# One block's weight panels in another order: four compression panels set between four recurrence panels, the compressed attention branch four panels later, and three openings and the last step rearranged

## The reference

```python
xn = rms_norm(x, norm1_w[l])
z = xn @ w_in[l]
(q, k_c, v_c, k_s, v_s, k_w, v_w, g_nsa, xr, gr, g_a, g_b) = jnp.split(z, IN_SPLITS, axis=-1)
attn = nsa_attention(q, k_c, v_c, k_s, v_s, k_w, v_w, gates, pos_k, pos_v, ck_w1, ck_w2, cv_w1, cv_w2)
rnn = rg_lru_branch(xr, gr, conv_w, conv_b, w_a, b_a, w_i, b_i, lam)
merged = sigmoid(g_a) * (attn @ w_up_attn) + sigmoid(g_b) * (rnn @ w_up_rnn)
x = x + merged @ w_out
x = x + square(relu(rms_norm(x, norm2_w) @ mlp_w1)) @ mlp_w2
```

## Time and profile before

| quantity | value |
|---|---|
| median of 3 runs | 981.76 us (981.12 to 982.61) |
| the profiled execution's own time | 982.4 us |
| its span | 980.6 us |
| PE busy | 956.8 us, 98% of the span |
| DVE busy | 657.8 us, 67% |
| ACT busy | 531.6 us, 54% |
| mean granted TensorE clock | 0.995 of full speed |

### The profile page before, as it was taken

How to read it: one execution, slowest core, us unless ns; L and a number is a source line. 1 busy time by engine, 2 the same in 40 slices (tenths; PEclk the granted TensorE clock), 3 DMA queues, 4 the chain that set the end, 5 groups by cost and what they waited for, 6 DMA issues and landing times.

```text
span 980.6 us, 15325 instructions
## 1 busy us (share of the span) xinstructions
PE 956.8 (98%) x6094; PEld 864.8 (88%) x6094; DVE 657.8 (67%) x841; ACT 531.6 (54%) x691; POOL 59.3 (6%) x92
## 2 busy tenths in 40 slices
PE   6999999999899999999999999999999999999997
PEld 6889999998788888888888888999999898888885
DVE  5976777865656655577656566868666676666664
ACT  6776668535444443475444445669663465454543
POOL 5000000000200000022221000100000020000000
PEclk9999999999899999999999999999999999999999
DMA  9773343655556565538676565454424556555541
GB/s 276 234 241 108 108 145 107 223 172 172 190 178 210 172 195 190 189 121 257 206 219 210 184 201 171 139 185 151 129 90 170 178 187 206 182 192 191 182 160 43
DMA packets 128674, 173.20 MB, mean 177 GB/s; under 512 B 3120, under 2 KB 111936, under 8 KB 128624
## 3 DMA queue, kind: packets, MB, share of 16 engines
q1 hardware_dynamic: 127232, 168.59, 53.8%
q0 software_dynamic: 1392, 3.91, 1.3%
HBM read 171.43 MB, written 1.05 MB: 176 GB/s over the span
## 4 chain that ended last, share of the span: by engine, by line
PE 53%; DVE 1%; ACT 0%; POOL 0%; issue 0%; POOLq 0%; ACTq 0%; DVEq 0%
PE pair L647 15%; PE pair L650 8%; PE acc L617 5%; PE acc L619 5%; PE acc L618 5%; PE pair L617 4%; PE pair L618 4%; PE pair L619 4%; PE acc L1072 1%; PE acc L1056 1%; PE acc L1048 0%; PE acc L1047 0%; POOL rstd L495 0%; DVE xt L1860 0%; PE pair L703 0%; PE pair L699 0%
## 5 line engine op out<-in xcount | busy, mean ns | idle before, releaser
L647 PE MATMUL pair<-actp,wh 128*128 128x512 f32 x912 | 295.0, 398 | 2.9 <-DVE arena L1890 2.7
L1556 DVE TENSOR_TENSOR wl<-raw,wh 128x2048 fp32r<-128x2048 f32 x89 | 203.8, 2290 | 68.4 <-ACT wh L1170 68.3
L1170 ACT ACTIVATE wh<-raw 128x2048 fp32r<-128x2048 f32 x88 | 168.3, 1912 | 85.7 <-PE acc L619 85.7
L650 PEld LDWEIGHTS pair<-actp,wl 128*128 128x128 f32 x912 | 172.7, 189 | 40.3
L617 PE MATMUL pair<-actp,wh 128*128 128x256 f32 x648 | 186.0, 287 | 1.0 <-DVE arena L1734 0.9
L618 PE MATMUL pair<-actp,wh 128*128 128x256 f32 x648 | 183.3, 283 | 0.0
L619 PE MATMUL pair<-actp,wl 128*128 128x256 f32 x648 | 183.2, 283 | 0.0
L650 PE MATMUL pair<-actp,wl 128*128 128x256 f32 x912 | 180.3, 279 | 0.0
L1164 ACT ACTIVATE wh<-raw 128x2048 fp32r<-128x2048 f32 x69 | 132.1, 1914 | 84.6 <-PE pair L619 57.3
L1551 DVE TENSOR_TENSOR wl<-raw,wh 128x2048 fp32r<-128x2048 f32 x68 | 155.5, 2288 | 32.6 <-ACT wh L1164 32.2
L647 PEld LDWEIGHTS pair<-actp,wh 128*128 128x128 f32 x912 | 142.9, 190 | 4.7 <-DVE wl L1551 2.9
(11 more groups left out here) (295 smaller groups left out, 1130.8 us busy)
## 6 DMA issues: line engine op xcount, KB each, us to landing
raw<-in_w_in SPq DMA_DIRECT2D x37, 1024.0 KB, 5.3
raw<-in_mlp_w SPq DMA_DIRECT2D x32, 1024.0 KB, 5.3
raw<-in_ffn_w_gate SPq DMA_DIRECT2D x22, 1024.0 KB, 5.3
raw<-in_ffn_w_up SPq DMA_DIRECT2D x22, 1024.0 KB, 5.3
raw<-in_ffn_w_down SPq DMA_DIRECT2D x22, 1024.0 KB, 5.0
raw<-in_w_out SPq DMA_DIRECT2D x8, 1024.0 KB, 4.9
raw<-in_w_up_rnn SPq DMA_DIRECT2D x4, 1024.0 KB, 5.1
raw<-in_cmp_k_w SPq DMA_DIRECT2D x2, 1024.0 KB, 7.3
```

Source lines behind the costliest of these rows:

```text
L647: return nc.tensor.matmul(bank[:, :].rearrange("p (u t) -> p u t", u=2), h[:, k, cs], actp[:, :, k, :], **kw)
L650: return nc.tensor.matmul(bank[:, 0:T], l[:, k, cs], acth[:, k, :], **kw)
L1170: nc.scalar.activation(wh[:, n % R, :], raw[:, n % R, :], ACT.Copy).then_inc(hi_ready, 1)
L1556: nc.vector.tensor_tensor(wl[:, n % R, :], raw[:, n % R, :], wh[:, n % R, :].bitcast(F32), ALU.subtract).then_inc(lo_ready, 1)
```

## The change

Block 1's panels 5 to 12 become XR, CK, XR, CK, XR, CV, XR, CV: a long one and a short one in turn. The heads stay at the same panel numbers (`HEADS` = 5), and so do the convolution and the recurrence (`CONV` = 12). The compressed branch moves from 9 to `CHAIN` = 13, each of its steps four panels later, and its output buffers move with it (`vblk` to `hidt`, `pc` and `pcT` elsewhere). The transposes of `atok` and the split of their result move from GA + 1 and GA + 2 to GB + 1 and GB + 2. On VectorE `lo(4)` moves behind `flat`, `lo(5)` behind the split of `flat`, `lo(6)` and `lo(7)` together at n = 5, `queries_lo` of the first half ahead of the constants of the recurrence, and three memsets go from n = 0 to n = 13 and 15.

Outside block 1: at the MLP's opening the copy stands ahead of `lo(ML + 2)`; `spread(3)` stands in the middle of panel QKV2 + 1; in the weighted `residual` the two early `norm_lo` stand behind the last half; in the last step ScalarE takes all four squares first, VectorE scales the tokens' halves 1 and 3 (the last one in one instruction from `xt`), ScalarE scales 0 and 2 and issues one output DMA.

The core of the diff:

```diff
-Q, KCVC, KSVS, KWVW, CK, CV, XR, GRP, GA, GB = 0, 2, 3, 4, 5, 7, 9, 13, 17, 21
+Q, KCVC, KSVS, KWVW, HEADS, GRP, GA, GB = 0, 2, 3, 4, 5, 13, 17, 21
+XRS, CMPS = (5, 7, 9, 11), (6, 8, 10, 12)
+CONV, CHAIN = 12, 13
...
-                if CK <= n < XR:
+                if n in CMPS:
...
-                if CK <= n < CK + NH:
-                    head_score(n - CK)
-                if n == CK:
+                if HEADS <= n < HEADS + NH:
+                    head_score(n - HEADS)
+                if n == HEADS:
...
-                if n in (XR + 6, XR + 7):
-
-                    tt = n - XR - 6
+                if n in (CHAIN + 6, CHAIN + 7):
+
+                    tt = n - CHAIN - 6
                     pe.wait_ge(pcT_ready, 1)
                     if tt:
                         pe.wait_ge(oc_read, 1)
...
-                if n == GA + 1:
+                if n == GB + 1:
                     pe.wait_ge(normed, NH)
...
             first_panel(QKV2, [FIRST2[:, c, :] for c in range(2)], 3)
-            spread(3)
...
                     if c == 1:
                         m.then_inc(panel_done, 1)
+                    elif n == QKV2 + 1:
+                        spread(3)
...
-            square_sum(5, apart=True, result=True)
...
+            square_sum(5, apart=True)
+            result(0, 1)
+            result(2, 3)
+            act.wait_ge(out_ready[2], 1)
+            act.dma_start(out[0, P:2 * P, 0:512], xs[:, 1, 0:512]).then_inc(stored, 16)
...
+            split_at = {KCVC: [], KSVS: [KWVW], KWVW: [], KWVW + 1: [KWVW + 2, KWVW + 3]}
...
-                if n < ML - 1:
-                    lo(n + 2)
-                if n == Q + 1:
+                for m in split_at.get(n, [n + 2]):
+                    if m <= ML:
+                        lo(m)
+                if n == Q:
                     queries_lo(qT, 0, 1)
-                if n == Q:
                     lru_constants()
+                if n == CHAIN:
                     link(nc.vector.memset(pc[:, :, :, :], 0.0))
-                    link(nc.vector.memset(vblk[:, :, :, :], 0.0))
                     link(nc.vector.memset(kcd[:, :, :], 0.0))
...
-                if n in (XR + 7, XR + 8):
-                    tt = n - XR - 7
+                if n in (CHAIN + 7, CHAIN + 8):
+                    tt = n - CHAIN - 7
                     dve.wait_ge(oc_done, tt + 1)
                     nc.vector.tensor_tensor(atok[:, tt, :], atok[:, tt, :], ps[7][:, :], ALU.add).then_inc(oc_read, 1)
                     dve.wait_ge(oc_read, tt + 1)
...
-                        if then is not None:
+                        if then is not None and not weighted:
                             norm_lo(r, then, range(2))
...
-            lo(ML + 2)
             done(ML)
             nc.vector.tensor_copy(ffr, pair01[:, :, 0:T]).then_inc(ff_sum, 2)
+            lo(ML + 2)
...
-            residual(5, END - 1, weighted=True, scaled=4)
-            dve.wait_ge(y_ready, 8)
-
...
+            last_half(0)
+            last_weighted(0)
+            last_half(1)
+            last_weighted(1)
+            last_half(2)
+            last_half(3)
+            dve.wait_ge(y_ready, 4 + 2)
+            dve.wait_ge(rstd_ready, TT * 5 + 1)
+            _, right = half_row(1)
+            nc.vector.tensor_scalar(xs[:, 0, right], xs[:, 0, right], rstd[:, 0:1], None, ALU.mult).then_inc(out_ready[1], 1)
+            last_weighted(2)
+            dve.wait_ge(x_summed, 4 * 4 + 4)
             dve.wait_ge(rstd_ready, TT * 5 + 2)
```

More of the change, by code:

```diff
@@ L346, in build @@
         vb_ready = sem("vb_ready")
-        out_ready = [sem(f"out_ready{tt}") for tt in range(TT)]
+        out_ready = [sem(f"out_ready{b}") for b in range(2 * TT)]
         stored = sem("stored")
@@ L461, in _ @@
             load_ffn(F2, a["ffn2_w_gate_2"][0], a["ffn2_w_up_2"][0], a["ffn2_w_down_2"][0])
-            for b in range(2 * TT):
+            for b in (1, 0, 3):
                 tt, cs = half_row(b)
-                sp.wait_ge(out_ready[tt], b % 2 + 1)
+                sp.wait_ge(out_ready[b], 1)
                 sp.dma_start(out[0, tt * P:(tt + 1) * P, cs], xs[:, tt, cs]).then_inc(stored, 16)
@@ L797, in heads_between, with bank1 @@
             def heads_between(n):
[L799 to L802, removed]
+                if 0 <= n - HEADS - 3 < NH:
+                    head_mix(n - HEADS - 3)
+                if 0 <= n - HEADS - 2 < NH:
+                    head_turn(n - HEADS - 2)
+            def bank1(n):
+                return ps[1 - XRS.index(n) % 2] if n in XRS else ps[n % 2]
             def free_bank(n):
@@ L1170, in hi_in_loop, with square_sum @@
                     nc.scalar.activation(wh[:, n % R, :], raw[:, n % R, :], ACT.Copy).then_inc(hi_ready, 1)
-            def square_sum(r, weighted=False, apart=False, result=False, halves=range(2 * TT)):
+            def square_sum(r, weighted=False, apart=False, halves=range(2 * TT)):
                 for b in halves:
                     tt, cs = half_row(b)
-                    if result and b == 3:
-                        act.wait_ge(rstd_ready, TT * r + 1)
-                        act.wait_ge(y_ready, 4 + 2)
-                        for c in (0, 1):
-                            _, c0 = half_row(c)
-                            nc.scalar.activation(xs[:, 0, c0], xs[:, 0, c0], ACT.Copy,
-                                                 scale=rstd[:, 0:1]).then_inc(out_ready[0], 1)
                     if r:
@@ L1273, in _ @@
                 hi(n + 2)
-                k = n - CK - 1
+                k = n - HEADS - 1
                 if 0 <= k < NH:
@@ L1871, in residual @@
                 if then is not None:
-                    norm_lo(r, then, range(2, KT))
+                    norm_lo(r, then, range(0 if weighted else 2, KT))
             def hidden_lo(s):
@@ L2116, in _, with last_half, last_weighted @@
             swiglu(F2, F2_F)
-            residual(5, END - 1, weighted=True, scaled=4)
-            dve.wait_ge(y_ready, 8)
+            def last_half(b):
+                tt, cs = half_row(b)
+                if b < 3:
+                    dve.wait_ge(bank_done, 3 * 4 + b + 1)
+                else:
+                    done(END - 1)
+                nc.vector.scalar_tensor_tensor(xt[:, tt, cs], acc4[:, b, :], late[:, tt:tt + 1], xt[:, tt, cs],
+                                               ALU.mult, ALU.add).then_inc(x_summed, 1)
+            def last_weighted(b):
+                tt, cs = half_row(b)
+                dve.wait_ge(x_summed, 4 * 4 + b + 1)
+                nc.vector.tensor_tensor(xs[:, tt, cs], xt[:, tt, cs], fnb[:, cs], ALU.mult).then_inc(y_ready, 1)
+            dve.wait_ge(late_ready, TT * 4)
+            dve.wait_ge(fnb_loaded, 16 * 2)
+            last_half(0)
[10 more added lines that the diff above has]
+            dve.wait_ge(x_summed, 4 * 4 + 4)
             dve.wait_ge(rstd_ready, TT * 5 + 2)
-            for b in (2, 3):
-                tt, cs = half_row(b)
-                nc.vector.tensor_scalar(xs[:, tt, cs], xs[:, tt, cs], rstd[:, tt:tt + 1], None, ALU.mult).then_inc(out_ready[tt], 1)
+            nc.vector.scalar_tensor_tensor(xs[:, 1, right], xt[:, 1, right], rstd[:, 1:2], fnb[:, right], ALU.mult,
+                                           ALU.mult).then_inc(out_ready[3], 1)
 _INS = ["x", "w_in", "cmp_k_w1", "cmp_k_w2", "cmp_v_w1", "cmp_v_w2", "lru_w_a", "lru_w_i", "w_up_attn", "w_up_rnn",
```

110 lines of the change are left out of this document (59 added, 51 removed).

## The result

| | before | changed |
|---|---|---|
| median | 981.44 us (981.12 to 982.61, 4 runs) | 988.27 us (987.92 to 990.2, 4 runs) |
| the profiled execution's own time / span | 982.4 / 980.6 us | 988.5 / 986.7 us |
| mean granted clock in it | 0.995 | 0.994 |

The changed kernel is slower: the medians differ by 6.8 us (a ratio of 1.0070), and the ratio that goes with the 95% interval is 1.0077 (1.0062 to 1.0091). 987.2 us were forecast. In a second group of runs it took 988.42 us against 980.89 (1.0080, interval 1.0067 to 1.0094).

The account below looks back on a forecast made before the run. TensorE, busy 956.8 of 980.6 us, was taken as the bound, so only its idle and slow time counted. Terms summed to +5.45 on the 981.76 us median, giving 987.2 us; range 982.6 to 990.4.

Parts of the forecast that it names:

- opening of block 1: Block 1's opening: TensorE's waits of 0.9, 1.4, 0.7 and 0.5 us go, leaving about 0.1: -3.4 us.
- mixes in panels 10 and 12: Short panels 10 and 12: each mix waits for a norm, a 2.99 us chain against 0.95 of cover: +4.1 us.
- panel 15: Compressed branch at n = 14: `gelu` and two table changes delay ScalarE 2.4 us, partly absorbed: +1.2 us.
- the addition: Output at n = 20: TensorE waits for VectorE's addition, behind `recur(0)` and `lo(22)`: +5.9 us, bounds 0 and 8.
- clock behind it: After the addition's wait: a slow stretch as after the profiled 2.7 us wait, +3.0 us, bounds 0 and 3.4.
- rival C: Clock also falls in the head waits of panels 10 and 12, once or twice: 990.2 to 993.2 us; 15%.
- MLP's opening and the spread: MLP: copy first, TensorE starts 1.8 us earlier, no 3.0 us clock loss, -4.8; `spread(3)`: wait moves to score, -0.15.
- residual and last step: Weighted residual -0.1 us; last step up to -0.8, less 0.2 for GpSimd's root beside VectorE, -0.6.
- Rival A: VectorE reaches the output's addition in time, so 5.9 and 3.0 us go: 978.3 us; 8%.
- E: No head waits in panels 10 and 12, VectorE's chain being shorter than 2.99 us: 983.1 us; 5%.
- Rival B: Clock does not fall after the 5.9 us wait for the addition: 984.2 us; 7%.
- Rival D: The MLP's opening still runs slow, adding 3.0 us: 990.2 us; 5%.

Follow-up runs that it names:

- the run with the wait of panel 12 alone: Changed kernel with the norm ahead of the mask on VectorE in panel 10 only, panel 12 keeping its wait: 989.93 us (one run).
- bank 6: Changed kernel with the second half of the compressed output in bank 6, so TensorE need not wait for the addition: 981.81 us, 1.0006 of before.
- both edits: Changed kernel with the compressed output's second half in bank 6 and each head's norm ahead of the mask on VectorE: 975.45 us, 0.9941 of before.

## Why the prediction was right, and where not

The forecast was the addition's wait with its slow stretch, 987.2 us; measured 988.27. Term by term, in the profiled executions:

| term | predicted | found |
|---|---|---|
| opening of block 1 | -3.4 | -3.5, all four waits gone |
| mixes in panels 10 and 12 | +4.1 | +4.1 (matmuls 2.05 late each, of which 1.88 is listed as a wait) |
| panel 13 | +0.3 | 0 |
| panel 15 | +1.2 | +0.9 |
| the addition | +5.9 | +5.7, and 0.2 for the first half of the output |
| clock behind it | +3.0 | +2.0 |
| clock behind a head wait (rival C) | 0 | +1.7 |
| block 1 together | +11.1 | +11.1 |
| MLP's opening and the spread | -4.8 and -0.15 | -1.8 for the wait, -2.9 from there to the first score of block 2 |
| residual and last step | -0.7 | -0.4 |
| span | +5.45 | +6.1 |

That block 1 came to 11.1 both times is luck in part: -1.0 for the clock behind the addition and -0.7 in small terms were made up by +1.7 that the sum put at 0.

**The places were right**, and two were shown by taking away what waits: 7.3 us for the addition with its clock, 5.8 for the two mixes with theirs. Rival A (the addition in time) and E (no head waits) fall. Rival B falls too: the clock did drop. Rival D falls: in the changed kernel the MLP's opening ran at 1.00. Rival C came true once of twice; the step "I take 0" for waits of 2.0 us was too low, by 1.7, and the run with the wait of panel 12 alone shows that it can be 3.4.

**The length of the addition's wait was right, both its ends were not.** The step was "the addition ends at 167.6" and TensorE would come at 161.7. In the trace the addition ends at 168.37 and TensorE has finished panel 20 at 162.80, 0.8 and 1.1 us later. The working took both times from the kernel before and left out what the sum's own terms do ahead of this place (-3.4 + 4.1 + 0.3 + 1.2 = +2.2 us for TensorE). Against the kernel before TensorE came 1.8 us later and the recurrence 0.15 later (159.37 for 159.22), where +0.7 and -0.6 were taken. That the difference still came out near 5.9 is partly luck.

**The clock terms were mis-sized.** The step was "I add the measured 3.0", from one stretch in one execution. The same wait was followed by a slow stretch of 6.8 us in that execution and of 3.4 in another. What a slow stretch costs depends also on how much of it the wait itself covers. Behind the addition the stretch had the same 6.8 us as in the earlier trace rows, but 2.8 of them were idle time, against 0.75 at the MLP's opening: 2.0 us lost instead of 3.0, and 2.9 where the wait was cut to 3.5. For the same reason the MLP's opening, -4.8 in the sum, was worth 3.1 in the times. The clock terms were off by -1.0 (addition), +1.7 (head wait) and, in the times, +1.7 (MLP); every other term came within 0.4.

**The term of the opening was right in size and wrong in one cause.** The step "with `flat` first it takes 30.4 to 33.7" described what happened, but it was not needed: with the split of panel 4 back ahead of it there was still no wait. The memsets that had left the opening gave VectorE the time, and the prediction does not name them.

**The last step.** 0.2 us was held back because GpSimd's root might be slowed by VectorE. It took 0.57 as before, but the two did not meet: VectorE's multiplication ended at 982.03 and the root began at 982.21. So the 0.2 were neither borne out nor refuted, and that the two engines hinder each other rests on the one row of 2.57 us. VectorE's last instruction ended 3.8 us after the start of TensorE's last matmul (979.86 to 983.63) instead of 4.6 (973.33 to 977.92). Of the 0.8 gained 0.4 reached the end. The other 0.4 went behind VectorE: the packets of the last two output DMAs, one on SyncE's queue and one on ScalarE's, ended at 985.91 and 985.75, 2.3 us after VectorE, where before the change it was 1.9 (979.84). Whether the second queue is the reason was not tried.

## What to carry to other kernels

When short and long units of work are alternated, list what waits in the middle of a unit: here a 3 us chain on VectorE that half a long panel hid stood open behind a short one. When a stage is moved by n turns, read what stands ahead of its small steps in the new turn: a 0.68 us addition that frees a bank cost 5.7 us behind the recurrence, and a second bank was the cure, while putting it forward by one instruction gained nothing measurable. Size a clock loss from several executions, not from one row.

## What the runs showed of the hardware

**The clock's loss does not follow the length of the wait.** The 14 traces have 15 slow stretches between the first panel and the last step. Each was at half clock for 3.4 us (seven) or for 6.8 us (eight), the idle time inside it counted. The 2.7 us wait at the MLP's opening was followed by 6.8 in one execution and 3.4 in the other, and the 1.9 us wait in panel 12 by 3.4 in five traces and 6.8 in one. The wait for the addition had 6.8 in all six traces, whether it was 5.7 or 3.5 us long. So a longer wait did not cost more clock, it cost less, because more of the stretch fell into it: 4.0 us of busy time at half clock behind 5.7 of idle time, 5.8 behind 3.5. And one stretch of 3.4 us stood where no wait exceeded 0.5. What decides between the two lengths stays open.

**A slow first panel.** In eight of the twelve profiles of the experiments (among them those with bank 6, with both edits, and of the kernel before once more) the first matmuls were 0.21 us apart instead of 0.12. The profile prints a granted clock of 1.00 there, but it has no record for this time. In the eight the first clock record (1.00) stands at 15.8 to 17.3 us, behind the first matmuls at 12.4 to 12.8; in the other four and in the first two profiles it stands at 10.9 to 12.1, ahead of them. And 0.21 us is the distance of 256-column matmuls in a stretch recorded at 0.50 (96.01 to 97.29 in the run with the wait of panel 12 alone). So the slow first panel ran at the lower level. It delayed the first score by 0.3 us in the kernel before, whose wait for `flat` absorbed most of it, and by 0.9 to 1.6 in the changed one (49.4 to 50.0 without it, 50.6 to 51.4 with it, against 49.77 in the first profile), which has no such wait. What sets the moment at which the clock rises stays open.
